# Hybrid attention layer on eight cores: the opening starts with the value projection, row block by row block, and the up weights are converted by two engines

## The reference

```
h    = rms_norm(x, g_pre)
proj = h @ w_in                      # 1024 x 5648: q_a k_a v_a z_a q_b k_b v_b z_b lr gate_a gate_b
oa   = diff_attention(q_a, k_a, v_a) # 4 heads, two 64-wide maps each, causal, ALiBi
ya   = (rms_norm(oa) * (1 - lam_init) * silu(z_a)) @ w_up_a
ob   = gated linear attention(q_b, k_b, v_b, decay from lr), chunked
yb   = (rms_norm(ob) * silu(z_b)) @ w_up_b
y    = sigmoid(gate_a) * ya + sigmoid(gate_b) * yb
out  = x + rms_norm(y @ w_out, g_post)
```

## Time and profile before

| | us |
|---|---|
| median of 3 runs | 1581.21 |
| lowest, highest | 1575.71, 1584.71 |
| the profiled execution | 1593.94 |
| span of its slowest core (core 6) | 1592.4 |
| spans of its eight cores | 1563.1 to 1592.4 |
| granted TensorE clock, core 6, mean | 0.958 |
| granted clock of the other cores | 0.963 to 0.981 |
| PE / ACT / DVE / POOL busy, share of the span | 90% / 53% / 45% / 30% |
| DMA, mean over the span | 130 GB/s |
| first 40 us: DMA share, rate | 0.90, 270 GB/s |

### The profile page before, as it was taken

The page is one execution under the profiler, slowest core; times in us unless marked ns, Lnnn a source line. Parts: engine busy times, 40 slices in busy tenths (PEclk is TensorE's granted clock), DMA queues, the critical chain, the costliest instruction groups (busy, mean ns, idle before and its releaser), DMA issues.

```text
span 1592.4 us, 27810 instructions; the slowest of 8 cores (1563.1 to 1592.4 us)
## 1 busy us (share of the span) xinstructions
PE 1431.3 (90%) x10576; PEld 746.3 (47%) x10576; DVE 712.3 (45%) x1453; ACT 850.7 (53%) x1714; POOL 476.5 (30%) x469
## 2 busy tenths in 40 slices
PE   4987798999889997999989998899998999999888
PEld 2443344544344543555445554455554555544443
DVE  3558745642556334643445324453233541233434
ACT  4254355234453546355664566746667557667632
POOL 1034422433325212433214322143211350220441
PEclk9989887889999998999999999999999999999999
DMA  8789686323442225322262222622225312215022
GB/s 270 222 228 261 167 283 212 126 86 116 154 168 93 95 91 198 107 88 99 94 225 68 94 80 94 225 67 76 85 80 186 97 64 67 80 67 186 28 76 110
DMA packets 75437, 207.43 MB, mean 130 GB/s; under 512 B 7984, under 2 KB 26672, under 8 KB 75312
## 3 DMA queue, kind: packets, MB, share of 16 engines
q1 hardware_dynamic: 75312, 205.66, 39.6%
HBM read 173.12 MB, written 32.51 MB: 129 GB/s over the span
## 4 chain that ended last, share of the span: by engine, by line
PE 69%; DVE 12%; ACT 8%; DMA 3%; POOL 3%; issue 3%; SPq 1%; DVEq 0%; POOLq 0%
PE ps_q L270 31%; PE ps_f L270 24%; PE ps_oa L270 13%; ACT sb_PT L999 3%; DMA sb_xb<-x 2%; DVE sb_scr L872 1%; DVE sb_scr L893 1%; ACT sb_junk L890 1%; DVE sb_wring L383 1%; ACT sb_ztmp L638 1%; DVE sb_rz L1025 1%; ACT sb_hb L589 1%; DVE sb_tmpo L1027 1%; DMA sb_V<-w_in 1%; DMA sb_KT<-w_in 1%
## 5 line engine op out<-in xcount | busy, mean ns | idle before, releaser
L999 ACT ACTIVATE sb_PT<-ps_q 128x512 bf16<-128x512 f32 (+3 forms) x697 | 359.8, 564 | 250.2 <-PE ps_q L270 153.9
L270 PE MATMUL ps_oa<-sb_V,sb_PT 128*128 128x129 bf16 x4224 | 345.7, 222 | 10.8 <-ACT sb_PT L999 4.9
L270 PEld LDWEIGHTS ps_oa<-sb_V,sb_PT 128*128 128x128 bf16 x4224 | 286.6, 99 | 139.9 <-issue 37.3
L999 ACT ACTIVATE sb_PT<-ps_f 128x512 bf16<-128x512 f32 (+3 forms) x455 | 247.0, 569 | 148.8 <-PE ps_f L270 84.8
L270 PE MATMUL ps_q<-sb_hT,sb_wring 128*128 128x512 bf16 x1048 | 265.2, 389 | 7.6 <-ACT sb_wring L379 3.8
L837 POOL TENSOR_TENSOR sb_yT<-sb_scr 128x512 bf16<-128x512 f32 x64 | 81.6, 1278 | 395.5 <-DVE sb_scr L835 395.3
L270 PE MATMUL ps_f<-sb_hT,sb_wring 128*128 128x512 bf16 x744 | 188.1, 386 | 5.6 <-DVE sb_qtT L698 1.6
L270 PE MATMUL ps_q<-sb_QT,sb_KT 64*128 64x512 bf16 (+3 forms) x697 | 155.8, 364 | 22.5 <-DVE sb_vb L688 9.3
L270 PE MATMUL ps_q<-sb_wring,sb_hT 128*128 128x512 bf16 x584 | 154.8, 402 | 14.3 <-ACT sb_PT L999 5.1
L270 PEld LDWEIGHTS ps_q<-sb_hT,sb_wring 128*128 128x128 bf16 x1048 | 95.4, 99 | 126.1 <-issue 51.3
L270 PE MATMUL ps_f<-sb_QT,sb_KT 64*128 64x512 bf16 (+3 forms) x455 | 128.4, 369 | 9.8 <-DVE sb_gaT L1062 3.8
(11 more groups left out here) (177 smaller groups left out, 1864.2 us busy)
## 6 DMA issues: line engine op xcount, KB each, us to landing
sb_wring<-wsc SPq DMA_DIRECT2D x204, 512.0 KB, 3.8
sb_xb<-x SPq DMA_DIRECT2D x60, 512.0 KB, 5.8
out<-sb_scr SPq DMA_DIRECT2D x32, 512.0 KB, 3.4
wsc<-sb_wring SPq DMA_DIRECT2D x30, 512.0 KB, 9.6
sb_KT<-w_in SPq DMA_DIRECT2D x48, 256.0 KB, 9.1
sb_V<-w_in SPq DMA_DIRECT2D x40, 256.0 KB, 8.7
sb_V<-w_out SPq DMA_DIRECT2D x8, 256.0 KB, 7.2
sb_KT<-w_out SPq DMA_DIRECT2D x8, 256.0 KB, 9.0
```

The source lines that it names most:

```text
L270: P.op("pe", lambda e: e.matmul(out=out_, lhsT=lhsT, rhs=rhs, start=start, stop=stop, **kw), reads=reads, writes=writes)
L999: act(lambda e, pp=pp, m=m, c0=c0, b=b, cbias=cbias: e.activation(out=PT[pp][:, m, c0:512], in_=BANK[b][:, c0:512], func=AF.Exp, bias=cbia ...
```

## The change

The opening loads VA first, then QA, then KA. The v chain of row block s of tile 0 stands directly behind the transposes of that block. Then come q of tile 0, v of tile 1 row block by row block in between, q of tile 1, the small constants, and k of both tiles last. A flag `ahead` keeps `tick` from writing conversions until tile 0's v is done. The table eft, which the v eviction multiplies by, is loaded at the start. For the up weights the constant factor is multiplied into two columns of `lams` in `setup_small` (two added 128x1 operations), so that `conv` may give every second one to ACT. Nothing else is changed: the chains, evictions, transposes and bytes are the same in number.

```diff
         x_load()
-        consts("sp", "cstA", [(ident[:], ident_d, "ident"), (smalls[:], smalls_d, "smalls")])
-        xst["limit"] = 4
-        x_load()
+        consts("sp", "cstA", [(ident[:], ident_d, "ident"), (smalls[:], smalls_d, "smalls"), (eft[:], ef_d, "eft")])
...
-                for n, (src, sc, c_) in enumerate(((w_up_a, smalls[:, 8:9], (1.0 - LAM_INIT) * 0.5), (w_up_b, smalls[:, 9:10], 0.5))):
+                for n, (src, sc, c_) in enumerate(((w_up_a, lams[:, 6:7], 1.0), (w_up_b, lams[:, 7:8], 1.0))):
...
-        wseq = QKV + SEQ_Z + SEQ_G
+        wseq = QKV[4:6] + QKV[0:4] + SEQ_Z + SEQ_G
...
-            if pend and pend[0][0] <= wst["acq"]:
+            if pend and pend[0][0] <= wst["acq"] and ahead[0]:
...
         emit_load()
         emit_load()
+        xlim(4)
         emit_load()
+        xlim(6)
         emit_load()
+        xlim(8)
+        a_stat(0, 0)
+        a_norm(0, 0)
         emit_load()
         emit_load()
+        consts("sp", "cstB", [...])
         emit_load()
+        take("VA0")
+        a_tr(0, 0)
+        take("VA1")
+        v_row(0, 0)
+        a_stat(0, 1)
+        a_norm(0, 1)
+        a_stat(0, 2)
+        a_tr(0, 1)
+        a_norm(0, 2)
+        v_row(0, 1)
+        a_stat(0, 3)
+        a_tr(0, 2)
+        a_norm(0, 3)
+        v_row(0, 2)
+        a_tr(0, 3)
+        v_row(0, 3)
+        take("QA0")
+        ahead[0] = True
+        q00 = pro_fm(0, "QA0", ev_q)
+        run_units(q00[0:2])
+        a_stat(1, 0)
+        run_units(q00[2:])
+        a_norm(1, 0)
+        a_stat(1, 1)
+        a_tr(1, 0)
+        a_norm(1, 1)
+        take("QA1")
+        q01 = pro_fm(0, "QA1", ev_q)
+        run_units(q01[0:2])
+        a_tr(1, 1)
+        v_row(1, 0)
+        a_stat(1, 2)
+        run_units(q01[2:])
+        a_norm(1, 2)
+        v_row(1, 1)
...
         release(2)
-        if two:
-            run_units(pro_fm(1, "KA", ev_k))
+        run_units(pro_fm(1, "QA0", ev_q) + pro_fm(1, "QA1", ev_q))
         release(2)
         setup_small()
-        run_units(tm_chunk([0, 1] if two else [0], QKV[4:6], ev_v))
+        take("KA0", "KA1")
+        run_units(pro_fm(0, "KA0", ev_k) + pro_fm(0, "KA1", ev_k) + pro_fm(1, "KA0", ev_k) + pro_fm(1, "KA1", ev_k))
+        release(2)
```

More of the change, by code:

```diff
@@ L346, in setup_small @@
             dve(lambda e: e.tensor_scalar(out=nbal[:], in0=smalls[:, 10:12], scalar1=-1.0, scalar2=None, op0=ALU.mult), ["smalls"], ["nbal"])
+            for c_, f_ in ((0, (1.0 - LAM_INIT) * 0.5), (1, 0.5)):
+                dve(lambda e, c_=c_, f_=f_: e.tensor_scalar(out=lams[:, 6 + c_:7 + c_], in0=smalls[:, 8 + c_:9 + c_], scalar1=f_, scalar2=None,
+                                                            op0=ALU.mult), ["smalls"], ["upsc"])
             dve(lambda e: e.tensor_copy(out=walpha[:], in_=walpha_st), ["ztmp"], ["walpha"])
@@ L373, in conv @@
         def conv(dst_ap, src_ap, stg, key, scale_ap, scale_c):
-            rd = [f"stg{stg}"] + (["smalls"] if scale_ap is not None else [])
+            rd = [f"stg{stg}"] + (["smalls", "upsc"] if scale_ap is not None else [])
             cctr[0] += 1
@@ L467, in _build @@
         calm = [False]
+        ahead = [False]
         def tick():
-            if pend and pend[0][0] <= wst["acq"]:
+            if pend and pend[0][0] <= wst["acq"] and ahead[0]:
                 for _ in range(4):
@@ L1073, in run_units, with take, xlim, pro_fm @@
                 f()
+        pst = {}
+        def take(*names):
+            for nm in names:
+                pst[nm] = acquire(nm)
+        def xlim(n):
+            xst["limit"] = n
+            x_load()
+        def pro_fm(t, nm, ev):
+            res = []
+            for jj in range(2):
+                res += fm_chain(t, lambda: pst[nm], jj, lambda b, jj=jj: ev(t, 2 * int(nm[2]) + jj, b))
+            return res
+        def v_row(t, s):
+            def one(b, k, st_, sp_):
+                sl = pst[f"VA{k // 4}"]
+                kk = k % 4
+                mm(BANK[b][:, :], hT[t % 2][:, k, s * 128:(s + 1) * 128], wring[:, sl, kk * 512:(kk + 1) * 512], st_, sp_,
+                   [f"w{sl}_{kk}", f"hT{t % 2}_{s}"], [b])
+            run_units(chain(8, one, lambda b: ev_v(t, s, b)))
@@ L1075, in _build @@
         emit_load()
         emit_load()
[L1077 to L1087, removed]
+        xlim(4)
         emit_load()
-        pst["QA0"] = acquire("QA0")
+        xlim(6)
         emit_load()
-        pst["QA1"] = acquire("QA1")
@@ L1093, in _build @@
-        two = ntiles > 1
-        a1 = a_units(1) if two else []
-        run_units(merge(pro_fm(0, "QA", ev_q), a1[0:5]))
+        xlim(8)
+        a_stat(0, 0)
+        a_norm(0, 0)
         emit_load()
-        pst["KA0"] = acquire("KA0")
         emit_load()
-        pst["KA1"] = acquire("KA1")
         consts("sp", "cstB", [(ztmp[:], w_alr, "ztmp"), (lamv_st, lamv_d, "oaf"), (tri[:], tri_d, "tri"), (negm[:], negm_d, "negm"),
-                              (eft[:], ef_d, "eft"), (rmask[:], rmask_d, "rmask")])
@@ L1102, in _build @@
-        run_units(merge(pro_fm(0, "KA", ev_k), a1[5:]))
+                              (rmask[:], rmask_d, "rmask")])
         emit_load()
-        if two:
-            run_units(pro_fm(1, "QA", ev_q))
+        take("VA0")
[12 more added lines that the diff above has]
+        v_row(0, 2)
@@ L1106, in _build @@
+        a_stat(1, 3)
+        a_tr(1, 2)
+        a_norm(1, 3)
+        v_row(1, 2)
+        a_tr(1, 3)
+        v_row(1, 3)
         release(2)
-        if two:
-            run_units(pro_fm(1, "KA", ev_k))
+        run_units(pro_fm(1, "QA0", ev_q) + pro_fm(1, "QA1", ev_q))
         release(2)
         setup_small()
-        run_units(tm_chunk([0, 1] if two else [0], QKV[4:6], ev_v))
+        take("KA0", "KA1")
+        run_units(pro_fm(0, "KA0", ev_k) + pro_fm(0, "KA1", ev_k) + pro_fm(1, "KA0", ev_k) + pro_fm(1, "KA1", ev_k))
```

## The result

| | before | after |
|---|---|---|
| median, us | 1579.87 (6 runs) | 1593.64 (6 runs) |
| lowest | 1575.71 | 1591.74 |
| ratio of the times | | 1.0084, 95% 1.0063 to 1.0105 |
| PE busy, share of the span | 90% | 88% |
| first chain of attention (q from sb_QT), mean of the eight cores | 76.96 us | 90.60 us |

The change makes the kernel slower: 13.8 us by the medians, 0.84% (13.3 us) by the ratio. One execution of before and two of after ran 3 to 8% longer than the others of their kernel, and the ratio leaves them out. The profiled execution of after took 1591.74 us at a granted clock of 0.978 on the core shown; that of before had 0.958, so the two spans (1590.2 and 1592.4) are not compared with each other. Points of the opening are: there each chain's own duration tells its pace, 1.89 us for one at full clock and up to 3.57 at half.

The account below looks back on a forecast made before the run. Opening bound by conversions and row blocks in engine order, its loss handed on: 24.8 start + 41.5 chains + 4.0 transposes + 14.4 idle + 6.0 half clock = 90.7, 15.7 later; less 1.5, +14.2 on 1581.21: 1595, range 1586 to 1602.

Parts of the forecast that it names:

- Start: Opening: row block 0's copy stands behind QA0's conversions on DVE, so the first v matmul comes at 24.8 us.
- Idle time of tile 0: Opening, tile 0's v rows: PE waits for evictions, normalisations and copies, idle 2.55, 1.25, 1.2 and 1.25 us.
- The stretch behind the first two q chains: Opening, before tile 1's first transposes: conversions, square, scaling, eviction and normalisation keep PE idle 4.3 us.
- Row blocks 2 and 3 of tile 1: Opening: late square and normalisation, then copies, leave PE idle 1.6, 1.1 and 1.2 us.
- Half clock: Opening: three chains and two sets of transposes run at half clock, mostly after idle stretches, costing 6.0 us.
- Handing on: Stages 0 and 1: bound by chains between engines, so the opening's 15.7 us loss passes on to the end.
- Rival 1: Later stages take the longer opening back, two thirds or more of 15.7 us: about 1580 to 1585; chance 0.18.
- Up weights: Stage 1: half of the 128x512 conversions go from DVE to ACT, returning 1.5 us.
- Range: Whole kernel: all terms at their bounds, QA0 landing 1.6 us earlier or 2 later included, give 1586 to 1602.
- Rival 2: Opening: v chains start at 16.1 us and idle stretches fall away, opening 11.7 us shorter, total 1568; chance 0.10.
- Rival 3: Opening: row-by-row start begins no earlier than before, 24.8 against 19.71 us; part of the forecast, no separate chance.

Follow-up runs that it names:

- e1: Changed kernel with QA0's load and conversions written behind tile 0's four v chains, DMA order kept; ratio to before 1.0038, attention starts at 84.6 us.
- e2: Changed kernel with tile 1's squares and normalisations ahead of the q chains and its transposes about one chain earlier; ratio to before 1.0050, attention starts at 83.9 us.
- e7: e5 with 18 dummy matmuls, results never read, ahead of its first v chain; ratio to before 0.9939, attention starts at 74.2 us.
- e3: Changed kernel with the edits of both e1 and e2; ratio to before 1.0005, attention starts at 78.1 us.
- e4: Kernel before with only the up weights' conversions changed, given to DVE and ACT in turn; ratio to before 0.9991, interval 0.9976 to 1.0005.
- e5: e3 with tile 0's row blocks also worked one step ahead and QA0's conversions released by the third and fourth v chains; ratio to before 0.9965.
- e8: e5 with tile 1's first square ahead of the third v chain and its normalisation behind QA0's conversions; ratio to before 0.9942, attention starts at 70.1 us.

## Why the prediction was right

1595 us was predicted and 1593.64 measured: +14.2 against +13.8. The steps are those that were forecast, but that the two numbers agree to 0.4 us is in part luck. On core 6 the opening is 14.6 us longer, where 15.7 was forecast: a later start (+1.4, the latest of the eight cores) stands against smaller idle and half clock terms (-2.3). In the mean of the cores it is 13.6 us longer. Less the up weights that would make 12.2, and 13.3 to 13.8 was measured. By the terms of the sum, core 6:

- **Start, 24.8 predicted, 26.16 measured on core 6 (+1.4), 24.37 in the mean of the cores.** (The prediction's own steps, landing at 23.6, 0.35 and 0.68, make 24.6.) The mechanism is shown by the copy at 25.34, and by e1, which takes it away. On core 6 the landing was mis-sized. By the windows 5.284 MB had been moved at 21.9 instead of 21.25, because the first 10 us moved 165 GB/s and not 194. The last chunk was converted 3.2 us behind that, instead of 2.3. The 358 GB/s of the Trainium skill ("DMA: Bandwidth & Descriptors", Specifications) would have put the landing at 19.1, an estimate; the last chunk was converted at 25.07, and only single windows of 2 us came near that rate (347 here, 272 in the next).
- **Idle time of tile 0: 2.55, 1.25, 1.2, 1.25 predicted; 2.35, 1.21, 1.09, 1.21 measured (-0.4).**
- **The stretch behind the first two q chains: 4.3 predicted, 3.36 measured (-0.9).** The steps came as listed, the square at 48.20, the sum's scaling at 49.37, an eviction, two conversions, the norm at 50.56. The sum of durations counted each to its end, and the rows overlap by about 0.1 at each step. e2 removed the stretch.
- **Row blocks 2 and 3 of tile 1: 1.6, 1.1, 1.2 predicted; 1.27, 0.88, 1.21 measured (-0.5).** Their causes are those named.
- **Half clock: three chains and two sets of transposes, as predicted;** the third chain was half slow only, 2.96 against 3.45 (-0.5). The reason given for it was weaker than it looked: in the kernel before, the 2.01 us stretch of the earlier trace rows stands on all eight cores, and the four matmuls behind it took 1.91 us on four of them (1, 2, 6 and 7) and 1.03 to 1.14 on the others.
- These make -0.9, and 90.7 less 89.6 is 1.1. The half clock and idle terms are not apart from the order: e7 shows that taking one away can lengthen the other.
- **Handing on:** the opening's 14.6 us on core 6 stand at 144.62 against 159.11. Over after, e1, e2, e3 and e4 the point where attention starts moved by 13.6, 7.6, 7.0, 1.2 and -0.1 us, and the time by the ratios by 13.3, 6.0, 7.9, 0.8 and -1.4, with intervals of 1.6 to 3.3 us on either side. Rival 1 is out.
- **Up weights: -1.5 predicted,** -1.43 by the two waits; for the whole time the interval of e4 includes zero, so the return is not shown there.
- **Range.** Its term for an earlier landing, 1.6 us, does not come out of its own working: 5.284 MB less 4.17, at 369 GB/s from 18 us on, ends at 21.02 instead of 21.25, 0.2 us earlier. With 0.2 the lower end would be 1588 instead of 1586.
- **Rival 2** had two conditions. e1, e3, e5 and e8 show that the start can be had: 14.36 to 16.31 on the cores listed, where 16.1 was worked out. The other, that the idle stretches fall away, needed the order rewritten (e5, e8). Its price was too high: e8 starts attention 6.8 us earlier than before and not 11.7, for its first row blocks still wait 1.16 and 0.47 and run slow, and small waits are left. Rival 3 held as part of the forecast, as it said.

## What to carry to other kernels

An instruction that converts a late transfer is a wait for everything behind it on its engine: read the order of each engine for what stands ahead of the first useful step, not only the order of the loads. When a projection is moved forward so that it can start on less data, count the chain that makes that data (square, scale, norm, transpose, copy) per step; if it is longer than the matmuls that it feeds, other matmuls must go between. A stretch taken away often comes back one station on, so put each step of the row chain one matmul chain ahead of its use, and write conversions after it.

## What the runs showed of the hardware

**Cores that issue the same loads get them at different times.** The last chunk of VA was converted at 14.14 us on core 5 of the changed kernel, at 15.59 on core 0 and at 17.18 on core 6, all eight cores loading. A core's own windows tell little of it: core 0 moved 163 GB/s in its first 10 us and core 6 moved 165, and then 303 against 288 up to 16 us, which makes up about 0.2 of the 1.6 us between them. The start of the first v chain scatters likewise, 23.75 to 26.16; in the kernel before the first q chain starts at 19.26 to 20.01. The count of bytes made here from one core's trace missed the mean of the cores by 0.4 us and that core by 1.4.

**The same idle stretch did not always bring half clock.** After 3.36 us the chain behind the transposes was slow on all eight cores of the changed kernel (2.89 to 3.52 us). In e1, after the same 3.36 us, it was at full speed on five of eight cores (1.89) and slow on three (2.91 to 3.00). After 2.01 us in the kernel before, half of the cores were slow. Shorter stretches were not safe either: in e1, with 1.27 and 0.88 us on the two sides of one row block's transposes and full-speed chains before them, the chain behind took 2.74 to 3.16 us on cores 0, 2, 3, 5 and 6. Those are the five that had been at full speed after 3.36 us; the three that had been slow there took 1.89 here. In the changed kernel, where all eight were slow after 3.36 us, the same two shorter stretches brought no slow chain on any. What decides stays open, but the length of the last stretch alone does not.

**The granted clock of the profile did not show the first slow chains.** On core 6 of the changed kernel it reads 1.00 from 26 to 38 us, while the chains at 26.16 and 34.31 took 3.57 and 3.38 us, a matmul about every 0.4 us. It reads 0.50 from 52 to 54 us, where the chain of 2.96 us stands. In the kernel before it reads 1.00 from 19 to 23, with a chain of 3.47 us, and 0.50 from 32 to 35. In the opening, then, the spacing of the matmuls has to be read and not this column alone.
